# Four norms of a two-block network: all tiles of the norm ahead of the product that waits for it, the shift's share of the raised slab on VectorE, and the squares of a norm in one tile

## The reference, cut to what matters

```
for l in range(2):
    h  = rms_norm(x, norm1[l]) * (1.0 + sc1) + sh1
    proj = h @ w_in[l]                       # q, k, v, g, u, vs, p, gates
    ...                                      # retention, spatial gating, pooling, branch products
    x  = x + gt1 * (merged @ w_out[l])
    h2 = rms_norm(x, norm2[l]) * (1.0 + sc2) + sh2
    hidden = square(relu(h2 @ w_ff1[l]))
    x  = x + gt2 * (hidden @ w_ff2[l])
return rms_norm(x, final_norm)
```

## Time and profile before

| | us |
|---|---|
| median of 3 runs (2671.29 to 2673.95) | 2673.62 |
| the profiled execution, its own time | 2668.45 |
| its span in the profile | 2666.6 |
| TensorE busy | 2606.2 |
| VectorE busy | 1507.1 |
| ScalarE busy | 1104.4 |
| GpSimd busy | 873.0 |

### The profile page before, as it was taken

How to read it: one execution, slowest core, us unless ns; L and a number is a source line. 1 busy time by engine, 2 the same in 40 slices (tenths; PEclk the granted TensorE clock), 3 DMA queues, 4 the chain that set the end, 5 groups by cost and what they waited for, 6 DMA issues and landing times.

```text
span 2666.6 us, 32706 instructions
## 1 busy us (share of the span) xinstructions
PE 2606.2 (98%) x13070; PEld 2140.6 (80%) x13070; DVE 1507.1 (57%) x1688; ACT 1104.4 (41%) x1296; POOL 873.0 (33%) x200
## 2 busy tenths in 40 slices
PE   7999889999999999999999999999999999999998
PEld 5776778888788888888888888888888888888887
DVE  5574537999764393263564336834563463735445
ACT  5453636877425432344332223435432343422222
POOL 0211020000242443454444444432443454444444
PEclk9999898999999999999999999999999999999999
DMA  4240026999221562233333333222652232233332
GB/s 153 103 151 1 1 102 238 365 365 356 69 101 48 200 258 95 95 103 111 111 108 120 123 123 108 96 93 81 242 199 88 102 118 85 105 126 124 120 124 107
DMA packets 61293, 361.14 MB, mean 135 GB/s; under 512 B 7280, under 2 KB 8176, under 8 KB 26096
## 3 DMA queue, kind: packets, MB, share of 16 engines
q1 hardware_dynamic: 58720, 353.49, 37.1%
q10 hardware_dynamic: 2448, 5.90, 0.6%
HBM read 357.25 MB, written 2.10 MB: 135 GB/s over the span
## 4 chain that ended last, share of the span: by engine, by line
PE 79%; DVE 5%; ACT 2%; issue 1%; POOL 0%; ACTq 0%; DVEq 0%
PE pd L272 19%; PE pd L273 19%; PE pd L274 19%; PE pd L296 2%; PE pd L297 2%; PE pd L298 2%; PE pd L2187 2%; PE pd L2189 2%; PE pd L2188 2%; DVE sb_y_lo L1913 2%; DVE sb_h_lo L562 1%; PE pd L2214 1%; PE pd L2216 1%; PE pd L2215 1%; PE pd L2144 1%
## 5 line engine op out<-in xcount | busy, mean ns | idle before, releaser
L226 POOL TENSOR_TENSOR sb_w_lo<-sb_raw,sb_w_hi 128x2048 fp32r<-128x2048 f32 x178 | 831.0, 4668 | 1667.8 <-ACT sb_w_hi L217 1667.8
L272 PE MATMUL pd<-sb_h_hi,sb_w_hi 128*128 128x512 f32 x1600 | 634.2, 396 | 3.9 <-DVE sb_h_lo L560 2.4
L274 PE MATMUL pd<-sb_h_hi,sb_w_lo 128*128 128x512 f32 x1600 | 623.7, 390 | 0.0
L273 PE MATMUL pd<-sb_h_lo,sb_w_hi 128*128 128x512 f32 x1600 | 623.7, 390 | 0.0
L217 ACT CAST sb_w_hi<-sb_raw 128x2048 fp32r<-128x2048 f32 x184 | 351.7, 1912 | 421.3 <-PE pd L274 324.6
L272 PE MATMUL pd<-sb_y_hi,sb_w_hi 128*128 128x512 f32 x960 | 376.4, 392 | 8.0 <-DVE sb_y_lo L1924 3.9
L273 PE MATMUL pd<-sb_y_lo,sb_w_hi 128*128 128x512 f32 x960 | 374.2, 390 | 0.0
L274 PE MATMUL pd<-sb_y_hi,sb_w_lo 128*128 128x512 f32 x960 | 374.1, 390 | 0.0
L272 PEld LDWEIGHTS pd<-sb_h_hi,sb_w_hi 128*128 128x128 f32 x1600 | 300.9, 188 | 72.7 <-issue 6.7
L274 PEld LDWEIGHTS pd<-sb_h_hi,sb_w_lo 128*128 128x128 f32 x1600 | 300.8, 188 | 63.5
L273 PEld LDWEIGHTS pd<-sb_h_lo,sb_w_hi 128*128 128x128 f32 x1600 | 301.0, 188 | 62.1 <-issue 1.9
(11 more groups left out here) (570 smaller groups left out, 3717.2 us busy)
## 6 DMA issues: line engine op xcount, KB each, us to landing
sb_raw<-in_slabs SPq DMA_DIRECT2D x190, 1024.0 KB, 4.8
sb_moe_raw<-in_moe SPq DMA_DIRECT2D x56, 1024.0 KB, 6.5
sb_raw<-in_moe SPq DMA_DIRECT2D x28, 1024.0 KB, 6.5
sb_QK<-in_ada SPq DMA_DIRECT2D x32, 512.0 KB, 5.4
sb_V<-in_ada SPq DMA_DIRECT2D x32, 512.0 KB, 5.6
sb_M<-in_ada SPq DMA_DIRECT2D x16, 512.0 KB, 4.0
sb_Y<-in_ada SPq DMA_DIRECT2D x16, 512.0 KB, 5.6
sb_MG<-in_ada SPq DMA_DIRECT2D x16, 512.0 KB, 5.7
```

What stands on the lines that cost most here:

```text
L226: pool.tensor_tensor(w_lo[j][:], raw[j][:], w_hi[j][:].bitcast(F32), ALU.subtract).then_inc(w_lo_ready[j], 1)
L272: pe.matmul(out, w_hi[j][:, cols], hi[:, k], start=(k == 0), stop=False)
L273: pe.matmul(out, w_hi[j][:, cols], lo[:, k], start=False, stop=False)
L274: last = pe.matmul(out, w_lo[j][:, cols], hi[:, k], start=False, stop=(k == KT - 1))
```

## The change: what it does

For norms 3, 4 and 5:

- The shift's share of the raised slab is computed by VectorE in float32 from the raw slab (`shift_sum`): one multiplication and seven multiply-adds of 128 x 256, each waiting for the one before, between the second and the third `add_to_x` of `add_raise`. What is left is a sum over partitions, two matmuls behind `spread_inverse` (`shift_total`). `shift_products`, `shift_keep` and `shift_turn` go. GpSimd waits for this sum before the remainder of the raised slab, which is what frees `raw[0]`.
- VectorE adds `sq[:, 7]` to `sq[:, 0]` too, so that TensorE has one tile to sum.
- `ahead_product` comes behind all eight tiles, and the third slab is handled in halves, as in norm 2: GpSimd subtracts after the last tile is ready, TensorE starts with the first half and waits for `ahead_out` alone.

For all four: ScalarE rounds the first half of the third slab ahead of tile 4 and the second half ahead of tile 6. In norms 2 and 4 the gain and the shift are read from `next_mod`, and the small operations that put them into `lay` go, but for one copy behind the norm.

```diff
         def norm_hi_part(act, u, sq, shift, slab_behind=None, slab_out_raised=None):
 
-            by_halves = u == 2 and slab_behind is not None
             for k in range(KT):
-                if k == 6 and by_halves:
+                if k == 4 and slab_behind is not None:
+                    act.wait_ge(raw_loaded[0], 16 * slab_behind + 16)
                     act.wait_ge(slab_done[0], slab_behind)
-                    split_front(act, slab_behind, 1)
+                    split_part(act, 0).then_inc(front_hi, 1)
                 elif k == 6 and slab_behind is not None:
-                    split(act, slab_behind, 0)
-                    slab_out_raised()
+                    split_part(act, 1).then_inc(w_hi_ready[0], 1)
...
                     pe.wait_ge(norm_merged, u - 1)
-                    token_sums(pe, sq[:, 0], True, False)
-                    pe.wait_ge(norm_sq, 4 * u + 4)
-                    token_sums(pe, sq[:, 7], False, True).then_inc(norm_sum, 1)
+                    token_sums(pe, sq[:, 0], True, True).then_inc(norm_sum, 1)
                 elif k == 3:
                     spread_inverse(pe, u)
-                elif k == 4:
-                    shift_products(pe, u - 2)
-            shift_turn(pe, u - 2)
+                    shift_total(pe, u - 2)
...
+        def shift_total(pe, e):
+
+            pe.wait_ge(shift_summed, e)
+            for f in range(2):
+                last = pe.matmul(px[1][:, f:f + 1], shift_row[:, f * P:(f + 1) * P], ones[:, 0:1],
+                                 start=(f == 0), stop=True, skip_group_check=True)
+            last.then_inc(shift_turned, 1)
...
+        def shift_sum(dve, v, m, e, shift):
+
+            dve.wait_ge(raw_loaded[0], 16 * m + 16)
+            part = lambda k: raw[0][:, k * SLAB_COLS:(k + 1) * SLAB_COLS]
+            v(dve.tensor_scalar(shift_row[:], part(0), shift(0), None, ALU.mult))
+            for k in range(1, KT):
+                ins = dve.scalar_tensor_tensor(shift_row[:], part(k), shift(k), shift_row[:], ALU.mult, ALU.add)
+                if k < KT - 1:
+                    v(ins)
+                else:
+                    v(ins, shift_summed, e)
...
                 raise_vector(dve, e, (2 * n, 2 * n + 1), hi, lo, gain)
+                if n == 1:
+                    shift_sum(dve, v, at + 2, e, shift)
...
             dve.wait_ge(half_sq, u - 2)
-            dve.tensor_tensor(sq[:, 0], sq[:, 0], sq[:, 6], ALU.add).then_inc(norm_merged, 1)
+            v(dve.tensor_tensor(sq[:, 0], sq[:, 0], sq[:, 6], ALU.add))
+            dve.wait_ge(norm_sq, 4 * u + 4)
+            dve.tensor_tensor(sq[:, 0], sq[:, 0], sq[:, 7], ALU.add).then_inc(norm_merged, 1)
...
-                if m is not None and u > 2 and step == 3:
-                    shift_keep(dve, u - 2)
-                elif m is not None and u > 2 and step == 6:
-                    ahead_product(dve, v, m, u - 2)
...
-            if m is not None and u == 2:
-                ahead_product(dve, v, m, 0)
+            if m is not None:
+                ahead_product(dve, v, m, u - 2)
...
                 if l:
+                    pool.wait_ge(shift_summed, 2 * l)
                     remainder(pool, L, 0)
                 remainder(pool, L, 1)
-                if l == 0:
-                    pool.wait_ge(h_ready, 8 * 2 + 8)
-                    remainder_front(pool, L + 1, 1)
-                else:
-                    remainder(pool, L + 1, 0)
+                pool.wait_ge(h_ready, 8 * (2 * l + 2) + 8)
+                remainder_front(pool, L + 1, 4 * l + 1)
...
-                with pool.Fori(L + L_FF, L + LAYER_PAIRS) as m:
+                pool.wait_ge(shift_summed, 2 * l + 1)
+                for j in range(2):
+                    remainder(pool, L + L_FF, j)
+                pool.wait_ge(h_ready, 8 * (2 * l + 3) + 8)
+                remainder_front(pool, L + L_FF + 1, 4 * l + 4)
+                remainder(pool, L + L_FF + 1, 1)
+                with pool.Fori(L + L_FF + 2, L + LAYER_PAIRS) as m:
...
-                dve.tensor_copy(lay[:, 0:V2_COLS], v2[:, bass.ds(l, 1)])
-                v(dve.tensor_tensor(lay[:, MOD:MOD + ADA_FIRST], b_ada[:, bass.ds(ADA_COLS * l, ADA_FIRST)],
-                                    mod[:, 0:ADA_FIRST], ALU.add))
-                v(dve.scalar_tensor_tensor(lay[:, GAIN:GAIN + 8], lay[:, MOD + 8:MOD + 16], 1.0, lay[:, 0:8],
-                                           ALU.add, ALU.mult), lay_ready, l + 1)
-                norm_vector(dve, v, 2 + 2 * l, O, lambda k: lv_(GAIN + k), lambda k: lv_(MOD + k), L)
+                norm_vector(dve, v, 2 + 2 * l, O, next_gain, lambda k: next_mod[:, k:k + 1], L)
+                v(dve.tensor_copy(lay[:, 0:V2_COLS], v2[:, bass.ds(l, 1)]))
```

More of the change, by code:

```diff
@@ L229, in build, with split_part @@
         FRONT = (slice(0, SLAB // 2), slice(SLAB // 2, SLAB))
+        def split_part(act, u):
+            return act.copy(w_hi[0][:, FRONT[u]], raw[0][:, FRONT[u]])
         def split_front(act, m, e):
             act.wait_ge(raw_loaded[0], 16 * m + 16)
-            act.copy(w_hi[0][:, FRONT[0]], raw[0][:, FRONT[0]]).then_inc(front_hi, 1)
-            act.copy(w_hi[0][:, FRONT[1]], raw[0][:, FRONT[1]]).then_inc(w_hi_ready[0], 1)
+            split_part(act, 0).then_inc(front_hi, 1)
+            split_part(act, 1).then_inc(w_hi_ready[0], 1)
         def remainder_front(pool, m, e):
@@ L334, in norm_hi_part @@
                 ins.then_inc(norm_hi, 1)
-            if by_halves:
+            if slab_out_raised is not None:
                 slab_out_raised()
@@ L441, in raise_vector, with shift_vector @@
                                          ALU.subtract).then_inc(ahead_lo, 1)
-        def shift_vector(dve, v, e, shift):
-            if e:
-                dve.wait_ge(shift_done, e)
+        def shift_sum(dve, v, m, e, shift):
[8 more added lines that the diff above has]
+                    v(ins, shift_summed, e)
+        def shift_vector(dve, v, shift):
             v(dve.tensor_copy(shift_parts[:, :, 0], shift))
@@ L463, in ahead_product, with add_raise @@
                 dve.tensor_tensor(T[:, f], pd[f][:], T[:, 2], ALU.mult).then_inc(ahead_out, 1)
-        def add_raise(dve, v, at, gate, u, sq, added, hi, lo, gain):
+        def add_raise(dve, v, at, gate, u, sq, added, hi, lo, gain, shift):
             e = u - 2
@@ L2280, in _ @@
                 slab_rows(pe, L, 1, h_hi, h_lo, (h_ready, 8 * (2 * l + 2)))
-                if l == 0:
-                    slab_rows_front(pe, L + 1, 1, h_hi, h_lo, (ahead_out, 2))
-                else:
-                    slab_rows(pe, L + 1, 0, h_hi, h_lo)
+                slab_rows_front(pe, L + 1, 4 * l + 1, h_hi, h_lo, (ahead_out, 4 * l + 2))
                 slab_rows(pe, L + 1, 1, h_hi, h_lo)
@@ L2383, in _ @@
                     if n:
-                        slab_rows_front(pe, L + L_POOL + n, 2 * l + 2, h_hi, h_lo)
+                        slab_rows_front(pe, L + L_POOL + n, 4 * l + 2, h_hi, h_lo)
                     else:
@@ L2387, in _ @@
                     pool_slab(n)
-                slab_rows_front(pe, L + L_Y2, 2 * l + 3, h_hi, h_lo)
+                slab_rows_front(pe, L + L_Y2, 4 * l + 3, h_hi, h_lo)
                 pe.wait_ge(y_ready, yb + Y_POUT + KT)
@@ L2399, in up_down @@
                     at = L + L_FF + 4 * q
-                    begin = 1 if isinstance(q, int) and q == 0 else 0
-                    for n in range(begin, 4):
-                        slab_rows(pe, at + n // 2, n % 2, h_hi, h_lo,
-                                  (h_ready, 8 * (2 * l + 3)) if begin and n == begin else None)
+                    if isinstance(q, int) and q == 0:
+                        slab_rows(pe, at, 1, h_hi, h_lo, (h_ready, 8 * (2 * l + 3)))
+                        slab_rows_front(pe, at + 1, 4 * l + 4, h_hi, h_lo, (ahead_out, 4 * l + 4))
+                        slab_rows(pe, at + 1, 1, h_hi, h_lo)
+                    else:
+                        for n in range(4):
+                            slab_rows(pe, at + n // 2, n % 2, h_hi, h_lo)
                     down_ready = (y_ready, yb + Y_FF + 8 * q)
```

22 lines of the change are left out of this document (13 added, 9 removed).

## The result

The changed kernel took 2657.92 us (median of 5 runs, 2656.71 to 2659.21), the kernel before 2671.29 us in the same comparison (5 runs, 2668.85 to 2673.95). The ratio is 0.995, 95% interval 0.9936 to 0.9965: faster by 9 to 17 us.

What follows compares the result with a forecast made beforehand. TensorE, busy 98% of the span, was taken as the bound. Gains of 9.6 us at norms 3 to 5, less 0.85 at norm 4, plus 0.55 at norm 2, make 9.3: 2673.62 to 2664.3 us, range 2661.5 to 2669.0.

Steps and rivals of the forecast that it cites:

- What bounds the kernel: Whole kernel: TensorE is busy for 98% of the span, so only shortening its list or its waits moves the end.
- the gain does not reach the end: Rival: something that does not move along, a load above all, holds TensorE in later parts; 2672 to 2674 us, chance 7%.
- The base: Starting time from which the gain was subtracted: the runs' median, 2673.62 us, 5.2 us above the profiled execution.
- The sum: Total gain behind the forecast: 9.6 us at norms 3 to 5, less 0.85, plus 0.55, making 9.3 us.
- shift, turn and wait of the three norms: TensorE at norms 3 to 5: shift products save 1.85 us, the turn 0.08, the wait for `h_lo` 0.38; 2.31 each.
- The shift sum: VectorE at norms 3 to 5: eight operations of 0.44 us, one held by GpSimd; at norm 3 it ends at 1308.1.
- costs what 512 columns cost: Rival: shift operations on VectorE take 0.72 us each, TensorE waits at norms 3 to 5; 2670.1 us, chance 11%.
- slower: Rival: VectorE becomes the bound in front of the raised slab, shift operations taking 1.6 us each; 2690.7 us, chance 4%.
- Norm 4's stall: TensorE at norm 4's raised slab waits 0.85 us for GpSimd's late remainder, the one loss counted.
- The eighth square: VectorE's extra sum of 0.69 us before the merge, hidden at norms 3 and 4; TensorE saves 0.89 us a norm.
- Tiles first: Norms 3 to 5: tiles made before the third slab's halves; the 0.38 us wait goes, all delays hidden, 2.1 us slack.
- Norm 2: ScalarE's casts placed apart let GpSimd start 0.66 us earlier, so TensorE begins the third slab sooner; gain 0.55 us.

## Why the prediction was off, point by point

**What bounds the kernel** was right: only TensorE's list and its waits moved the end, and nothing behind 670 us gave anything back ("the gain does not reach the end" falls).

**The base was the step that failed most.** The prediction says "The terms are steps of one list and hold there too" and takes 9.3 us from the 2673.62 of the runs. The terms do hold there, but the number was no typical run: it was the median of three of which two lay in the upper cluster, and the mean of 80 is 2670.7. That is 2.9 of the 6.4 us. Taken from the profiled execution's own 2668.45, the same sum gives 2659.2, which is the mean of the changed kernel's 21 runs to 0.1 us; but that is luck, since that base lies 2.2 us under the mean and the sum is 2.3 us short of the difference of the means. The range's lower end, "no stall and a run or two lower", allowed 2.8 us for runs that scatter by 7.

**The sum was 1.2 us short**, and all of it lies in the shift, turn and wait of the three norms (1.19; the other terms cancel to 0.03). The turn and the wait were priced by the step that they lengthen, and not by the one behind. These rows of TensorE before stand behind the turn and behind the wait:

```profile
1334.29 0.40 PE L273 MATMUL pd<-sb_h_lo,sb_w_hi 128*128 128x512 f32 x1
...
1341.61 0.40 PE L273 MATMUL pd<-sb_h_lo,sb_w_hi 128*128 128x512 f32 x1
```

Each is 0.34 us behind the matmul ahead of it (1333.95 and 1341.27) and not 0.23. With these 0.11 us each, 2.31 becomes 2.53; the raised slab itself became 2.92 us shorter and not 2.82 (0.08 of that is the step ahead of the turn, from 1333.11 to 1333.42, which was not counted either), and that makes 2.63 of the 2.70 measured. The wait was worth 0.38 + 0.11 = 0.49, and taken away alone it gave 0.50.

**The remaining 2.3 us** are the five first runs, 1.2 us under the mean of 21, and 1.1 us between the trace (10.5) and the means (11.6, interval 10.7 to 12.4). The medians of the four sets were 13.4, 12.5, 12.2 and 10.9 us apart, so a real effect in the first 670 us is neither shown nor ruled out, and whether the 1.1 us is chance stays open. The last norm's end scatters too: 2.73 to 3.92 us for its one group in the four traces of the changed kernel.

**The shift sum** went as worked out. The operations took 0.485 us each where 0.44 was interpolated, one of them 4.71; the sum ended at 1308.4, which is the forecast's 1308.1 and the 0.33 us by which this run was late, and cost TensorE nothing at norms 3 and 5, though with only 0.36 us to spare at norm 3. The rivals "costs what 512 columns cost" and "slower" fall. **Norm 4's stall** was 0.77 us. The forecast says 0.85, but its own times, 1674.65 less 1673.88, make 0.77; the 0.08 on top has no row. With two operations earlier it is gone, so the cause is the one named.

**The eighth square** was hidden, and at norm 3 as counted: the merge was through at 1321.85 and TensorE asked at 1322.24. At norm 4 it was hidden for a reason that the prediction does not have. It checked the merge alone. Behind the merge stood the three small operations on `lay`, which it does not mention; without their removal this edit costs 5.7 us at norm 4 and eats its own gain. As far as the prediction goes, that the changed kernel escaped this is luck.

**Tiles first** was called hidden and worth the wait. It is more: ScalarE's halves and GpSimd's late start cost nothing (third slab at 1342.24, its first half ready at 1340.1), and without this part the shortened list runs into the held tile, which costs 2 us of wait and 1.6 us of clock. The forecast credited the shift's 1.93 us and the wait's 0.38 as separate terms; they hold only together. Which piece of this part does it (the order of the tiles, ScalarE's halves or GpSimd's late start) was not run apart; the rows of the shift alone, with the tile held for as long as the remainder runs, point to GpSimd's start.

**Norm 2** gave 0.48 of 0.55, and in part at another place. The forecast had it all at the third slab, with TensorE's own slab ending "little before that". These rows of TensorE before stand in that slab, at its seventh tile:

```profile
718.71 0.39 PE L274 MATMUL pd<-sb_h_hi,sb_w_lo 128*128 128x512 f32 x1
719.24 0.50 PE L272 MATMUL pd<-sb_h_hi,sb_w_hi 128*128 128x512 f32 x1
719.58 0.40 PE L273 MATMUL pd<-sb_h_lo,sb_w_hi 128*128 128x512 f32 x1
```

The steps of 0.53 and 0.34 us are 0.41 us over the pace, and in the changed kernel both are 0.23. Only 0.09 us came off the step into the third slab. With that wait in place TensorE could not have begun the third slab ahead of 722.10 (its last start before it, 721.87, and 0.23), so a half that is ready sooner would by itself have given 0.29 us there and 0.11 behind. The prediction does not say that ScalarE's new order takes away this wait as well; that the size came out is partly luck.

## What to carry to other kernels

Subtract a worked-out gain from the mean of many runs, and let the range carry the scatter of runs; three runs are too few where single runs differ by 7 us. Taking work off the bounding engine moves it towards waits that were just hidden: ask at each place where the list gets shorter which producer does not move with it. Before an operation is pushed later on VectorE, look for a GpSimd instruction that starts within the stretch by which it moves, and at every small operation up to the next one that TensorE needs.
